# A four-layer mixer kernel: the first layer's dt block and first input block multiplied in the setup phase, its first B and C block split there

## The chip, the cores and the metric

The kernel runs on one core of one Trainium2 chip. The metric is the device time of one execution in microseconds (us), here the median of three. A core has five engines with queues of their own: TensorE multiplies matrices, VectorE, ScalarE and GpSimd work on elements, SyncE mostly issues transfers (DMA). The instructions of one engine run in order; the engines meet only at semaphores. In profile rows they are PE (PEld is its weight load), DVE, ACT, POOL and SP. A row with a q behind the engine, as SPq, is an instruction of its queue, such as the issue of a transfer.

## The reference

One prompt of 256 tokens and 8 samples of 4 tokens (288 columns in all) go through four layers. A layer is a root-mean-square norm, a mixer and a gated feed-forward part. The mixers are a state-space mixer (ssd), sliding-window attention, differential attention, and ssd again. The change touches only what comes before the first mixer and that mixer's start:

```python
for layer in range(DEPTH):
    hp = rmsnorm(xp, norm_mix[layer]); hs = rmsnorm(xs, norm_mix[layer])
    if kind == 0:                      # layers 0 and 3
        proj = h @ ssm_w_in            # z, x, B, C and dt columns: 2048 + 2048 + 512 + 512 + 32
        # causal convolution of width 4 over x, B, C, then silu; dt through softplus;
        # a state update per head from state_ssm; gate with z; norm; ssm_w_out
    x = x + mixer(h)
    x = x + swiglu(rmsnorm(x, norm_ffn[layer]), ffn_w_in[layer], ffn_w_out[layer])
```

All of it is float32. The kernel gets near that precision with numbers split in two: a rounded high part and the rest, so each product is three matmuls (high by high, low by high, high by low).

## The kernel before

The program is a row of phases. A phase ends when all five engines have reached its end, and the next begins with all of them together. The first is `setup`, then each layer has one phase or more.

Activations lie transposed: `x` is 8 chunks of 128 model features by 288 columns. `prepare` makes of each chunk the high part `xh` (ScalarE, L330) and the low part `xl` (VectorE, L336), and GpSimd adds up the squares in `acc` (L343 to L348). The norm's factor is applied behind the matmuls: `rstd` sums `acc` over the partitions on TensorE (L356) and ScalarE makes `rx` of it (L361, L365).

Weights come in blocks, numbered through the program. A block of 1 MB (0.5 MB for block 0) is loaded in two transfers into one of two buffers `raw` (L218), ScalarE rounds it into `whi` (`split_hi`, L229) and VectorE makes the rest `wlo` (`split_lo`, L240); `whi` and `wlo` have two buffers too. TensorE runs over it with `block_pieces`: 32 matmuls with `whi` (L268, 16 for block 0), then 16 with `wlo` (L276, 8 for block 0). The load of block g waits until the low part of block g-2 is made, the split of block g until TensorE is done with block g-2. All waits stand in the order of the code; nothing is scheduled by a program.

The first ssd layer takes its blocks in this order: 0 is the dt columns, 1 the first block of x, 2 to 5 the B and C columns, 6 the next of x, then z and x in turn. Between blocks TensorE does small work: `rs_pe` (L356), 24 transposes of the old convolution state (L951, of the tile `strow`), the transposes of dt (L957) and two products of the heads' constants (L960, L962). `strow` lies in the same memory as the first of the four state buffers `H`. So SyncE waits for `strow_turned`, which comes with the last of the 24 transposes, before it issues the four loads of `H` (512 KB each, L894), and behind these in its queue stand the loads of block 4 and block 5.

VectorE takes in this layer, in this order: three memsets (L1530 to L1532); dt scaled out of PSUM (L1538, which also frees PSUM bank 0 by the signal `out_read`); small work on constants; the old convolution state `stT` (L1551, waits for the 24 transposes); block 1 scaled into the convolution's buffer (L1509, L1511); the transposed dt (L1556); the low part of block 3; the convolution's taps (L1524); the softplus of dt; block 2 scaled; the low part of block 4 (L240); the rest of softplus up to `dsk` (L1581). With `dsk` TensorE may start the sums over tokens (L971), which stand in its queue ahead of block 4.

In `setup`, SyncE loads the table of constants `cst` (500 KB, with the identity in its first 128 columns) and the input `xt`, then blocks 0 and 1, then small rows of gains and convolution weights. TensorE waits for all of constants and input, transposes the input chunk by chunk (L635), then the rows (L641), then makes four distance tables (L650, each one matmul of 512 columns on 33 rows), which VectorE copies (L699) and SyncE stores. Last comes a small product whose copy is `lamcol` (L653, L713).

## Time and profile before

| what | us |
|---|---|
| median of 3 runs | 2025.04 |
| lowest and highest | 2024.25 and 2027.71 |
| the profiled execution | 2020.47 |
| its span | 2018.5 |
| TensorE busy | 1882.3 (93%) |
| VectorE busy | 1171.5 (58%) |
| ScalarE busy | 981.2 (49%) |
| GpSimd busy | 498.3 (25%) |

The span runs from the first instruction to the last; the profiled execution's own time is 2.0 us more. Times in rows count from the start of the span. Setup takes the first 32 us of it, the first layer's mixer begins there.

### The profile page before, as it was taken

The numbers are of one execution on the slowest core, as the hardware profiler recorded it, in microseconds if no ns is written. First come the engines' busy times: TensorE is split into PE (matmuls) and PEld (weight loads), VectorE is DVE, ScalarE is ACT, GpSimd is POOL, SyncE is SP. The second block draws the span as 40 slices with busy tenths as digits, with TensorE's granted clock in tenths as the row PEclk, the third lists the DMA queues.
The fourth block names the chain that finished last, engine by engine and source line by source line (L and its number), as shares of the span: only waits on it lengthen the run. The fifth ranks groups of instructions, "written<-read, shape, count | busy, mean of one in ns | idle before, by whom it ended". The sixth has DMA issues, their size and how long they took to land. (4 is left out here: it accounts for less than half of the span.)

```text
span 2018.5 us, 37752 instructions
## 1 busy us (share of the span) xinstructions
PE 1882.3 (93%) x14726; PEld 1770.9 (88%) x14726; DVE 1171.5 (58%) x2048; ACT 981.2 (49%) x1639; POOL 498.3 (25%) x521
## 2 busy tenths in 40 slices
PE   6899969999999979999897878999998999799999
PEld 4899959999998769999895658999988999699998
DVE  4678864555444356554446765555475888555544
ACT  3677763444343334443443554444347777544432
POOL 3122302343102113431103302343111222023320
PEclk9999979999999889999998998999998999799999
DMA  6367855555575536555657724655562787466544
GB/s 176 115 215 244 263 182 155 164 162 155 159 214 156 164 109 179 163 149 158 195 174 264 270 87 137 172 163 155 160 203 94 232 257 239 126 167 167 166 142 133
DMA packets 501554, 352.65 MB, mean 175 GB/s; under 512 B 14729, under 2 KB 486203, under 8 KB 500603
## 3 DMA queue, kind: packets, MB, share of 16 engines
q1 hardware_dynamic: 493508, 304.52, 52.0%
q0 software_dynamic: 7440, 45.43, 6.2%
q8 instruction: 118, 1.93, 0.4%
q14 instruction: 58, 0.48, 0.1%
q10 hardware_dynamic: 430, 0.29, 0.1%
HBM read 326.58 MB, written 50.63 MB: 187 GB/s over the span
## 5 line engine op out<-in xcount | busy, mean ns | idle before, releaser
L268 PE MATMUL ps<-xh,whi 128*128 128x288 f32 x2368 | 654.7, 302 | 10.1 <-PEq L176 9.9
L240 DVE TENSOR_TENSOR wlo<-raw,whi 128x2048 fp32r<-128x2048 f32 (+3 forms) x241 | 501.9, 2083 | 247.5 <-ACT whi L229 247.3
L268 PE MATMUL ps<-xl,whi 128*128 128x288 f32 x2368 | 643.8, 298 | 0.0
L229 ACT ACTIVATE whi<-raw 128x2048 fp32r<-128x2048 f32 (+3 forms) x241 | 419.1, 1740 | 265.8 <-PE ps L276 220.0
L268 PEld LDWEIGHTS ps<-xh,whi 128*128 128x128 f32 x2368 | 452.0, 191 | 12.7 <-issue 10.6
L268 PEld LDWEIGHTS ps<-xl,whi 128*128 128x128 f32 x2368 | 452.7, 191 | 0.8
L276 PE MATMUL ps<-xh,wlo 128*128 128x288 f32 x2368 | 353.2, 300 | 0.0
L276 PEld LDWEIGHTS ps<-xh,wlo 128*128 128x128 f32 x2368 | 327.1, 189 | 1.1
L526 POOL TENSOR_TENSOR gh<-sg,ut 128x288 f32<-128x288 f32 x88 | 216.2, 2457 | 353.1 <-ACT sg L467 353.1
L268 PE MATMUL ps<-hh,whi 128*128 128x288 f32 x704 | 189.7, 296 | 0.0
L268 PE MATMUL ps<-hl,whi 128*128 128x288 f32 x704 | 189.6, 297 | 0.0
L469 ACT ACTIVATE hh<-gh 128x288 fp32r<-128x288 f32 x88 | 39.2, 445 | 225.9 <-POOL gh L526 225.9
L268 PE MATMUL ps<-oh,whi 128*128 128x288 f32 x400 | 114.6, 312 | 33.2 <-DVE ol L399 18.1
L330 ACT ACTIVATE xh<-x,vec 128x288 fp32r<-128x288 f32 x64 | 33.9, 536 | 204.6 <-DVE x L486 123.0
L268 PEld LDWEIGHTS ps<-hl,whi 128*128 128x128 f32 x704 | 132.6, 188 | 0.0
L268 PEld LDWEIGHTS ps<-hh,whi 128*128 128x128 f32 x704 | 132.4, 188 | 0.0
L1230 POOL TENSOR_TENSOR E<-E,cb 128x288 f32<-128x288 f32 x64 | 58.5, 915 | 248.1 <-ACT E L1391 239.3
L268 PE MATMUL ps<-ol,whi 128*128 128x288 f32 x400 | 113.8, 309 | 0.0
L268 PEld LDWEIGHTS ps<-oh,whi 128*128 128x128 f32 x400 | 80.9, 202 | 35.5 <-issue 35.5
L276 PE MATMUL ps<-hh,wlo 128*128 128x288 f32 x704 | 104.2, 296 | 0.0
L503 DVE TENSOR_TENSOR hl<-gh,hh 128x288 fp32r<-128x288 f32 x88 | 40.3, 458 | 103.4 <-ACT hh L469 103.4
L345 POOL TENSOR_TENSOR sqx<-x 128x288 f32<-128x288 f32 x56 | 39.7, 710 | 245.6 <-DVE x L509 151.1
(326 smaller groups left out, 2658.2 us busy)
## 6 DMA issues: line engine op xcount, KB each, us to landing
raw<-in_ffn_w_in SPq DMA_DIRECT2D x176, 512.0 KB, 5.1
raw<-in_ssm_w_in SPq DMA_DIRECT2D x80, 512.0 KB, 5.2
raw<-in_ffn_w_out SPq DMA_DIRECT2D x64, 384.0 KB, 4.0
raw<-in_ffn_w_out SPq DMA_DIRECT2D x64, 320.0 KB, 3.2
H<-in_state_ssm SPq DMA_DIRECT2D x32, 512.0 KB, 4.6
out_ssm_sample<-H SPq DMA_DIRECT2D x32, 512.0 KB, 7.2
raw<-in_ssm_w_out SPq DMA_DIRECT2D x32, 512.0 KB, 5.3
Kp_L<-in_cache_diff_k SPq DMA_DIRECT2D x64, 256.0 KB, 4.5
```

The costliest lines, as they stand in the source:

```text
L229: act.activation(wts["hi"][:, s, 0:width], raw[:, s, 0:width], ACT.Copy).then_inc(hi_ready.sem, 1)
L240: dve.tensor_tensor(wts["lo"][:, s, 0:width], raw[:, s, 0:width], wts["hi"][:, s, 0:width].bitcast(F32), ALU.subtract).then_inc(lo_ready.s ...
L268: pe.matmul(out, W[0][:, kk, j, :], x_[:, k, :], stop=False, start=(part == 0 and kk == 0 and x_ is seg.hi), skip_group_check=True)
L276: mm = pe.matmul(out, W[1][:, kk, j, :], seg.hi[:, k, :], start=False, stop=(part == parts - 1 and end), skip_group_check=True)
L330: act.activation(th[:, c, :], x[:, c, :], ACT.Identity, scale=vec[:, 0, gain + c:gain + c + 1]).then_inc(xh_ready.sem, 1)
L345: pool.tensor_tensor(sqx[:, c % 2, :], x[:, c, :], x[:, c, :], ALU.mult).then_inc(sq_done.sem, 1)
L469: act.activation(hh[:, i, :], gh[:, r, :], ACT.Copy).then_inc(hid_hi.sem, hid_hi.inc())
L503: dve.tensor_tensor(hl[:, i, :], gh[:, r, :], hh[:, i, :].bitcast(F32), ALU.subtract).then_inc(hid_lo.sem, hid_lo.inc())
L526: pool.tensor_tensor(gh[:, r, :], sg[:, r, :], ut[:, r, :], ALU.mult).then_inc(gated_ready.sem, gated_ready.inc())
L1230: pool.tensor_tensor(E[:, h % 4, :], E[:, h % 4, :], cb[:, h // 8, :], ALU.mult).then_inc(w_ready.sem, w_ready.inc())
```

## The change

Setup gives the identity a transfer of its own, ahead of all; the input comes in two halves of 512 features, each with its own semaphore, and the rest of the constants behind the weights of blocks 0 and 1. The six small loads of `perhead` go from ScalarE's queue to SyncE's (`heads_in`). ScalarE loads its table of functions before the first chunk. TensorE then multiplies block 0 and block 1 in setup, with three of the tables between them and the norm's sum inside block 1; the fourth table, the transposes of the rows and `lamcol` come behind. ScalarE copies the tables in VectorE's place, makes `rx` and the high part of block 2; VectorE makes the low parts of blocks 0, 1 and 2. SyncE loads blocks 2 and 3 in setup. The first layer starts with block 2, and the 24 transposes and those of dt stand inside it. Layer 3 goes as before. The blocks' descriptions move out of `ssd` into `ssd_segs`, unchanged.

```diff
     def setup(nxt):
         stream["prep"] += 1
         prep_act, prep_dve, prep_pool = prepare(0, V_MIX)
+        rs_pe, rs_act, _ = rstd(stream["norm"])
+        opened = ssd_segs(0)
+        dt_seg, bc_seg, x_seg = opened
+        half, wide = D_MODEL // 2, 2 * KD * P
...
-            x_in = [(cst[:, :], A["constants"])]
-            x_in += [(xt[:, t, :], A["x_prompt"][0, t * P:(t + 1) * P, :]) for t in range(2)]
-            x_in.append((xt[0:NS, 2, :], A["x_sample"].rearrange("b t d -> (b t) d")))
+            x_in = []
+            for h in range(2):
+                cols = slice(h * half, (h + 1) * half)
+                x_in.append([(xt[:, t, cols], A["x_prompt"][0, t * P:(t + 1) * P, cols]) for t in range(2)])
+                x_in[h].append((xt[0:NS, 2, cols], A["x_sample"].rearrange("b t d -> (b t) d")[:, cols]))
...
             def _(sp):
-                for dst, src in x_in:
-                    sp.dma_start(dst, src).then_inc(x_loaded.sem, x_loaded.inc())
+                sp.dma_start(cst[:, 0:P], A["constants"][:, 0:P]).then_inc(ident_in.sem, ident_in.inc())
+                for h in range(2):
+                    for dst, src in x_in[h]:
+                        sp.dma_start(dst, src).then_inc(half_in[h].sem, half_in[h].inc())
                 for i in range(2):
                     load_block(sp, nxt, i, i, wait=False)
-                for dst, src in rows_in:
+                sp.dma_start(cst[:, P:], A["constants"][:, P:]).then_inc(cst_in.sem, cst_in.inc())
+                for dst, src in rows_in + heads_in:
                     sp.dma_start(dst, src).then_inc(rows_loaded.sem, rows_loaded.inc())
+                load_block(sp, bc_seg.lin, 0, 2)
                 sp.wait_ge(tab_moved.sem, tab_moved.at(4))
                 sp.dma_start(dist_tab.rearrange("k h n -> h k n"), tab[:, :, :]).then_inc(
                     tab_stored.sem, tab_stored.inc())
+                load_block(sp, bc_seg.lin, 1, 3)
...
+                block_mm(pe, dt_seg, 0)
+                pe.wait_ge(loaded.sem, loaded.at(len(rest_in)))
+                pe.wait_ge(made2.sem, made2.at(1))
+                for k in range(3):
+                    table(k)
+                L = block_pieces(pe, x_seg, 0)
+                for _ in range(KD):
+                    next(L)
+                pe.wait_ge(cst_in.sem, cst_in.at(1))
+                rs_pe(pe)
+                for _ in L:
+                    pass
+                pe.wait_ge(tab_moved.sem, tab_moved.at(1))
+                table(3)
...
                 for n in range(3):
-                    pe.transpose(ps[:, n, 0:used[n]], rows[0:used[n], n, :],
+                    pe.transpose(ps[:, 1, P * n:P * n + used[n]], rows[0:used[n], n, :],
                                  ident[0:used[n], 0:used[n]]).then_inc(turned.sem, turned.inc())
...
+                roots_table(act)
                 act.wait_ge(moved.sem, moved.at(1))
                 for c in range(KD):
                     act.wait_ge(turned.sem, turned.at(c + 2))
                     act.activation(x[:, c, :], ps[:, 3 + c % 4, 0:TOK], ACT.Copy).then_inc(x_done.sem, 1)
                     prep_act(act, c)
-                for i in range(2):
-                    split_hi(act, i, nxt.width if i else nxt.first_width)
+                split_hi(act, 0, nxt.first_width)
...
+                split_hi(act, 1, nxt.width)
+
+                def move_table(k):
+                    act.wait_ge(tab_made.sem, tab_made.at(k + 1))
+                    act.activation(tab[:, k, :], ps[0:NH, 4 + k % 3, :], ACT.Copy).then_inc(tab_moved.sem, tab_moved.inc())
+
+                for k in range(3):
+                    move_table(k)
+                rs_act(act)
+                move_table(3)
+                split_hi(act, 2, wide)
...
+                for n in range(3):
+                    lo = 0 if n else 32
+                    dve.tensor_copy(vec[:, n, lo:used[n]], ps[:, 1, P * n + lo:P * n + used[n]]).then_inc(
+                        moved.sem, moved.inc())
+                split_lo(dve, 2, wide)
...
-                for m in range(2, 4):
+                for m in range(2, 2 if opened else 4):
                     seg, i = block_of(m)
                     load_block(sp, seg.lin, i, b0 + m)
...
+                if opened:
+                    L = block_pieces(pe, bc_seg, 0)
+                    more(L, 4)
+                    turn_rows()
+                    more(L, 4)
+                    turn_dt()
+                    rows_of_heads()
+                    more(L, KD + 1)
+                else:
+                    block_mm(pe, dt_seg, 0)
+                    rs_pe(pe)
+                    turn_rows()
+                    block_mm(pe, x_seg, 0)
+                    turn_dt()
+                    rows_of_heads()
+                    block_mm(pe, bc_seg, 0)
...
-                rs_act(act)
+                if not opened:
+                    rs_act(act)
...
-        setup(firsts[0])
-        for layer in range(DEPTH):
+        opened = setup(firsts[0])
+        ssd(0, firsts[1], opened)
+        for layer in range(1, DEPTH):
             kinds[layer](layer, firsts[layer + 1])
```

TensorE at the boundary between setup and the first layer, before. The rows are the end of block 0 (`wlo`), the norm's sum, the transposes of `strow` (in the memory of `H`) and the first of block 1:

```order
L945 UNCONDITIONAL_BRANCH [waits barrier_Pool_Activation_PE_DVE_SP_release]
L268 MATMUL ps<-xh,whi 128x288 [waits x_lo_ready,weights_hi_ready]
...
L276 MATMUL ps<-xh,wlo 128x288 [waits weights_lo_ready]
L276 MATMUL ps<-xh,wlo 128x288 x7
L356 MATMUL ps<-acc,cst 128x288 [waits squares_added]
L951 MATMUL ps<-cst,H 128x24 [waits strow_in]
```

And in the changed kernel, where the first block of this phase is block 2:

```order
L680 MATMUL ps<-lw,cst 128x1 [waits moved,made]
L176 UNCONDITIONAL_BRANCH
L990 UNCONDITIONAL_BRANCH [waits barrier_Pool_Activation_PE_DVE_SP_release]
L268 MATMUL ps<-xh,whi 128x288 [waits x_lo_ready,weights_hi_ready,outs_read]
L268 MATMUL ps<-xl,whi 128x288
...
L995 MATMUL ps<-cst,H 128x24 [waits strow_in]
L995 MATMUL ps<-cst,H 128x24 x23
L268 MATMUL ps<-xh,whi 128x288 [waits x_lo_ready]
```

Ahead of the 24 transposes stood 24 matmuls of block 0 and the norm's sum; now 16 matmuls of block 2 stand there, and the first of these waits for `outs_read` (the signal `out_read`).

SyncE at the same boundary, before; `H` is first `strow`, then the states:

```order
L888 UNCONDITIONAL_BRANCH [waits barrier_Pool_Activation_PE_DVE_SP_release]
L890 DMA H<-in_state_ssm_conv 24x3072
L218 DMA raw<-in_ssm_w_in 128x4x256 [waits weights_lo_ready]
L218 DMA raw<-in_ssm_w_in 128x4x256
L894 DMA H<-in_state_ssm 128x8x128 [waits strow_turned]
L894 DMA H<-in_state_ssm 128x8x128 x3
```

And in the changed kernel, from the last small loads of setup on:

```order
L627 DMA perhead<-in_ssm_d 32x1 x2
L218 DMA raw<-in_ssm_w_in 128x4x256 [waits weights_lo_ready]
L218 DMA raw<-in_ssm_w_in 128x4x256
L630 DMA dist_tab<-tab 12x4x512 [waits tables_moved]
L933 UNCONDITIONAL_BRANCH [waits barrier_Pool_Activation_PE_DVE_SP_release]
L935 DMA H<-in_state_ssm_conv 24x3072
L939 DMA H<-in_state_ssm 128x8x128 [waits strow_turned]
L939 DMA H<-in_state_ssm 128x8x128 x3
L218 DMA raw<-in_ssm_w_in 128x4x256 [waits weights_lo_ready]
```

The loads of blocks 2 and 3 have gone ahead of the boundary; the states still wait for the 24 transposes, and block 4 still stands behind the states.

## Rows read from the trace of the kernel before

**Rows 1.** Head of the page: span and count.

```profile
span 2018.5 us, 37752 instructions
```

**Rows 2.** Waits of TensorE, 0 to 110 us: us, times, longest.

```profile
PE ps L630 <- DMA xt<-in_x_sample: 10.5, 1, 10.5
...
PE ps L971 <- DVE dsk L1581: 1.0, 1, 1.0
```

**Rows 3.** Busy per engine in stretches; then TensorE clock, DMA share, GB/s.

```profile
0.00:6.00 6.00, 0.00 (x0) 0.00 (x0) 0.13 (x2) 0.00 (x0) 0.20 (x4) 1.00 0.66 192
0.00:10.50 10.50, 0.01 (x1) 0.01 (x1) 0.15 (x3) 0.00 (x0) 0.20 (x4) 1.00 0.86 231
```

**Rows 4.** Timeline of setup: start us, us, engine, line, out<-in, count.

```profile
10.73 6.95 PE L635 MATMUL ps<-cst,xt 128*128 128x128 f32 x24
...
11.75 1.28 ACT L665 ACT_TABLE_LOAD   x1 [11.75 <-PE ps L635]
...
13.04 0.41 ACT L665 ACTIVATE x<-ps 128x288 f32<-128x288 f32 x1
...
17.87 0.83 PE L641 MATMUL ps<-cst,rows 101*128 101x101 f32 x3 [0.18 <-DMA rows<-in_diff_k_norm]
...
19.98 2.84 ACT L229 ACTIVATE whi<-raw 128x1024 fp32r<-128x1024 f32 x2
...
20.86 0.59 DVE L694 COPY vec<-ps 128x69 f32<-128x69 f32 x3
...
21.22 6.98 PE L650 MATMUL ps<-oh,rb 33*12 33x512 f32 x8 [2.52 <-DVE vec L694]
...
28.24 0.68 DVE L699 COPY tab<-ps 12x512 f32<-12x512 f32 x1 [1.03 <-PE ps L650]
...
31.80 0.16 DVE L713 COPY lamcol<-ps 128x1 f32<-128x1 f32 x1 [0.67 <-PE ps L653]
```

**Rows 5.** Timeline of the first layer's start, all engines.

```profile
32.42 0.58 PE L268 MATMUL ps<-xh,whi 128*128 128x288 f32 x1 [0.66 <-PEq L176]
...
33.20 0.91 DVE L1532 MEMSET Bm<- 32x1024 f32 x1 [0.16 <-issue]
...
36.36 1.22 PE L276 MATMUL ps<-xh,wlo 128*128 128x288 f32 x8
...
38.00 1.67 PE L951 MATMUL ps<-cst,H 24*128 24x24 f32 x24
...
39.11 0.46 DVE L1538 TENSOR_TENSOR G<-ps,rx 32x288 f32<-32x288 f32 x1 [5.00 <-ACT rx L365]
...
41.01 2.29 DVE L240 TENSOR_TENSOR wlo<-raw,whi 128x2048 fp32r<-128x2048 f32 x1 [0.75 <-ACT whi L229]
```

**Rows 6.** Timeline of SyncE's transfers, 39 to 47 us.

```profile
39.70 5.36 SPq L894 DMA_DIRECT2D H<-in_state_ssm  x4
45.10 2.60 SPq L218 DMA_DIRECT2D raw<-in_ssm_w_in  x2
```

**Rows 7.** Timeline of VectorE and ScalarE, 47 to 61 us.

```profile
47.05 0.21 DVE L1556 COPY G<-ps 128x64 f32<-128x64 f32 x1
...
53.97 1.92 ACT L229 ACTIVATE whi<-raw 128x2048 fp32r<-128x2048 f32 x1 [4.43 <-DMA raw<-in_ssm_w_in]
...
55.92 2.29 DVE L240 TENSOR_TENSOR wlo<-raw,whi 128x2048 fp32r<-128x2048 f32 x1
...
60.63 0.17 DVE L1581 COPY dsk<-ps 128x16 f32<-128x16 f32 x1
```

**Rows 8.** Stretches as in rows 3, later in the layer.

```profile
42.00:54.00 12.00, 12.00 (x94) 11.73 (x94) 9.17 (x17) 3.20 (x5) 0.77 (x4) 1.00 1.08 299
64.00:65.00 1.00, 1.00 (x6) 1.00 (x6) 1.00 (x3) 0.71 (x2) 0.68 (x1) 0.50 0.00 0
```

**Rows 9.** Timeline of TensorE, block 4.

```profile
63.44 0.48 PE L268 MATMUL ps<-xh,whi 128*128 128x288 f32 x1
...
69.32 2.32 PE L276 MATMUL ps<-xh,wlo 128*128 128x288 f32 x16
```

More of the change, by code:

```diff
@@ L707, in _ @@
                     made.sem, made.inc())
+                split_lo(dve, 0, nxt.first_width)
+                for q in range(2):
+                    rows_ = slice(32 * q, 32 * q + 32)
+                    dve.tensor_copy(id2[rows_, :], ident[rows_, rows_]).then_inc(filled.sem, filled.inc())
+                dve.tensor_copy(id2[2 * HEADS:P, :], ident[2 * HEADS:P, 0:HEADS]).then_inc(filled.sem, filled.inc())
                 dve.wait_ge(made.sem, made.at(3))
@@ L711, in _ @@
                     in1=lw[:, 2 * HD + 2:2 * HD + 3], op0=ALU.add, op1=ALU.subtract).then_inc(made.sem, made.inc())
+                split_lo(dve, 1, nxt.width)
+                dve.wait_ge(cst_in.sem, cst_in.at(1))
+                for q, (at, n) in enumerate(((C_TRI, P), (C_TRI, P), (C_TRIS, NS))):
+                    dve.tensor_scalar(after[:, q * P:q * P + n], cst[:, at:at + n], -1.0, -NEG, ALU.add,
+                                      ALU.mult).then_inc(filled.sem, filled.inc())
+                for n in range(3):
+                    dve.wait_ge(turned.sem, turned.at(KD + n + 2))
+                for n in range(3):
+                    lo = 0 if n else 32
+                    dve.tensor_copy(vec[:, n, lo:used[n]], ps[:, 1, P * n + lo:P * n + used[n]]).then_inc(
+                        moved.sem, moved.inc())
+                split_lo(dve, 2, wide)
                 dve.wait_ge(turned.sem, turned.at(KD + 5))
-                dve.tensor_copy(lamcol[:, :], ps[:, 7, 0:1]).then_inc(moved.sem, moved.inc())
+                dve.tensor_copy(lamcol[:, :], ps[:, 1, 500:501]).then_inc(moved.sem, moved.inc())
+        return opened
     def finish():
@@ L758, in ssd_first, with conv_of, ssd_segs, ssd @@
         return Linear(2, KD, 2, lambda i, slot: first(0, slot) if i == 0 else rest(i - 1, slot), KD * P)
-    def ssd(layer, nxt):
+    def conv_of(s):
+        return 4 + s if s else 0
+    def ssd_segs(layer):
+        w, early, b0 = A["ssm_w_in"][layer // 3], 4, stream["block"]
+        n_x, scaled = stream["prep"] - 1, S("xb_scaled")
+        at = lambda k: 8 * n_x + k + 1
+        dt = Seg(Linear(1, KD, 1, columns(w, KD, 1, col0=SSM_IN - P)), xh, xl, xl_ready, at,
+                 lambda o: (out_read, out_read.at(1)), places=[b0], banks=lambda i, j: 0)
+        bc = Seg(Linear(early, KD, 2, columns(w, KD, 2, col0=2 * D_INNER)), xh, xl, xl_ready, at,
+                 lambda o: (scaled, scaled.at(2 * (1 + o // 2) + 2)),
+                 places=[b0 + 2 + i for i in range(early)], banks=lambda i, j: 2 * (i % 2) + j)
+        xs = Seg(Linear(CI // 2, KD, 2, columns(w, KD, 2, col0=D_INNER)), xh, xl, xl_ready, at,
+                 lambda o: (scaled, scaled.at(2 * conv_of(o // 2) + 2)),
+                 places=[b0 + 1] + [b0 + 2 + early + 2 * i for i in range(CI // 2 - 1)],
+                 banks=lambda i, j: (2 if i == 0 else 0) + j)
+        return dt, bc, xs
+    def ssd(layer, nxt, opened=None):
         i_ssd = layer // 3
@@ L956, in _ @@
-                for t, n in TILES:
-                    mm = pe.transpose(ps[0:n, 6, 32 * t:32 * t + 32], dtT[:, cols_of(t)], ident[0:HEADS, 0:HEADS])
-                mm.then_inc(dt_turned.sem, dt_turned.inc())
-                pe.wait_ge(a_diag.sem, a_diag.at(2))
-                pe.matmul(ps[:, 7, 96:128], ones[0:HEADS, :], ea[:, 1:1 + HEADS], start=True, stop=True)
-                for h in range(2):
-                    mm = pe.matmul(ps[64 * h:64 * h + 64, 7, P:P + CI], ones[0:HEADS, 0:64], Dd[:, h, :],
-                                   start=True, stop=True)
@@ new lines, in rows_of_heads, with more @@
+                def rows_of_heads():
+                    pe.wait_ge(a_diag.sem, a_diag.at(2))
+                    pe.matmul(ps[:, 7, 96:128], ones[0:HEADS, :], ea[:, 1:1 + HEADS], start=True, stop=True)
+                    for h in range(2):
+                        mm = pe.matmul(ps[64 * h:64 * h + 64, 7, P:P + CI], ones[0:HEADS, 0:64], Dd[:, h, :],
+                                       start=True, stop=True)
+                    mm.then_inc(rows_mm.sem, rows_mm.inc())
+                def more(L, n=1):
+                    for _ in range(n):
+                        next(L, None)
@@ L1111, in turn_tail @@
                     mm.then_inc(tl_mm.sem, tl_mm.inc())
-                def more(L, n=1):
-                    for _ in range(n):
-                        next(L, None)
                 L = block_pieces(pe, *block_of(2 + EARLY))
```

87 lines of the change are left out of this document (30 added, 57 removed).

## The prediction

> **What bounds the kernel now.** I read the head of the page, then the waits of TensorE in the first 110 us, then timelines. The change touches only setup and the start of the first layer, so nearly all of the 2018.5 us span [rows 1] is out of its reach: it can only shift what comes behind it. TensorE waits 10.5 us for constants and input, and the only other wait in the stretch up to 61 us that the layer itself makes is 1.0 us for `dsk` at L971 [rows 2]. That small wait is the important one. TensorE is busy from 32.4 to 60 us, but where it arrives it still waits for VectorE, so the time of `dsk`, 60.63 + 0.17 = 60.8 us [rows 7], sets all that follows. Any gain has to come through `dsk`; TensorE's work ahead of it was nearly covered.
>
> What sets `dsk`? VectorE goes from the transposed dt at 47.05 to 60.8 without a long break [rows 7]. On the way stands the low part of block 4 at 55.92, which starts 0.03 us after its high part (53.97 + 1.92 = 55.89), and ScalarE began that one when the load of block 4 landed, after 4.43 us of idling for it [rows 7]. So there are two chains of nearly equal length: VectorE's own, and the transfer of block 4. The second begins with the 24 transposes: they end at 38.00 + 1.67 = 39.67, SyncE issues the four states at 39.70 and block 4 at 45.10 [rows 6], and block 4 is there at 53.97. From 42 to 54 us the DMA engines move 299 GB/s at a share over 1 [rows 8], which is 3.59 MB; four states and block 4 are 2.10 + 1.05 = 3.15 MB. This chain is filled by bytes, and takes 14.3 us from the end of the transposes (53.97 - 39.67).
>
> **The change, step by step.** I work out when the 24 transposes end, since block 4 follows by 14.3 us.
>
> *Input in halves.* All inputs, and the three tables on ScalarE's queue, are 1.92 MB; they were complete at 10.5 us, when 231 GB/s x 10.5 = 2.43 MB had moved [rows 2, 3]. Identity, first half and the same tables are 0.92 MB; with the same surplus (2.43/1.92) they are in when 1.16 MB have moved, and 192 x 6.0 = 1.15 MB had by 6.0 us [rows 3]. So transposing starts at 6.0 in place of 10.73 (bounds 5.3 and 7.5). The second half has until 9.5 and costs nothing. The function table, 1.28 us ahead of the first copy, is now loaded before. First copy: 6.0 + (13.04 - 10.73 - 1.28) = 7.0. ScalarE took from 13.04 to 19.98 for the eight chunks [rows 4]: done at 14.0. High part of block 0: about a third of 2.84 [rows 4], done at 14.9.
>
> *Block 0.* It took 32.42 to 36.36 for 16 matmuls, 0.246 us each [rows 5], at the half clock (at 63.44 to 69.32 block 4 shows the same pace until the clock comes back [rows 9], and there the clock column reads 0.50 [rows 8]; ahead of 60 us it reads 1.00 even at this pace, so I go by the pace). Here it again comes after transposes, which did not raise the clock before. 14.9 + 3.9 + 1.2 = 20.0.
>
> *Three tables.* Eight passes took 6.98 us at the half clock [rows 4]: three tables are 5.2, or 2.6 at the full clock. Then block 1: 32 matmuls are 5.9 when the clock must first come back, as for block 4 [rows 9], or 4.3 at the full clock; the norm's sum 0.7; 16 more 2.2 [rows 9]. I take the tables at 2.6, since dense work precedes them, and block 1 from the half clock: its end is 20.0 + 2.6 + 5.9 + 0.7 + 2.2 = 31.4 (29.8 if all is at full clock, 34.0 if neither is).
>
> *Tail of setup.* Fourth table 0.9; its copy, on ScalarE now, 0.6 (VectorE took 0.68); the high part of block 2 stands behind it, 1.9; its low part 2.3 [rows 5, 7]; `lamcol` 0.2, and 0.46 from its end at 31.96 to the first matmul of the layer at 32.42 [rows 4, 5]. The transposes of the rows (0.83) and their copies (0.59) [rows 4] run beside ScalarE's part. Sum 6.3, so the layer starts at 37.7 in place of 32.4. The small loads moved to SyncE's queue land long before they are needed.
>
> *Start of the layer.* Block 2 wants PSUM bank 0, which held dt; it is free when VectorE has scaled dt out, behind its three memsets. These ended 33.20 + 0.91 = 34.11, and scaling takes 0.46 [rows 5]: 2.2 us after the start. TensorE has then idled for some 5 us and begins at the half clock: 16 matmuls 3.9, then the 24 transposes 1.7. They end at 37.7 + 2.2 + 3.9 + 1.7 = 45.5, against 39.67: 5.8 us later.
>
> *What follows.* Blocks 2 and 3 are loaded early, but this takes no byte off the chain, because states and block 4 still start only behind the transposes and the earlier loads had just run dry when the states' data began. Block 4 lands at 45.5 + 14.3 = 59.8, its low part starts at 61.8, VectorE needs from there 60.8 - 55.92 = 4.9 to `dsk`: 66.6 in place of 60.8. VectorE's own chain would be ready sooner: dt transposed about 2.5 us behind the 24 transposes, at 48.0, and 13.3 us to `dsk` (13.75 less its short wait for block 3), 61.3. TensorE comes to L971 about 57 and now idles for some 9 us. Behind L971 every step takes its input from steps that have shifted alike, so I carry the shift to the end undiminished: +5.8.
>
> The load of block 5 is issued right behind block 4 now, since the low part of block 3 is long done. If the two shared the engines equally, block 4 could lose up to 1.5 us; if not, nothing. Before, 3.59 MB moved in 42 to 54 us where 3.15 were needed [rows 8], so some sharing was there already. The Trainium skill (DMA: Bandwidth & Descriptors, "Two DMAs through the same engine are not ordered") says that within one queue of one DMA engine descriptors start in order. By this rule block 5 takes nothing from block 4 and the shift stays; by the other bound it would be 1.5 us more. The surplus in the row stands for a mixture, and I add nothing.
>
> The sum is made against the profiled execution: 2020.47 + 5.8 = 2026.3. The median of the runs is 2025.04, 4.6 us above that execution; on it I expect **2030.9 us**, 0.29% slower.
>
> **Rivals.** *The transfer is not what is late.* If states and block 4 come 5 us faster than before from a queue that is empty, VectorE's own chain decides: `dsk` at 61.3, +0.5, or 2025.5. For it: VectorE's chain was as long as the transfer's. Against it: 3.15 MB in 9 us would be 350 GB/s from the first byte, and the stretch shows 299.
>
> *Faster: TensorE's queue decides.* Block 2 started at about 47 before (as dt was transposed, [rows 7]) and now at 37.7 + 2.2; the transposes inside are 1.7 + 0.8 and the slow clock 1.8, so TensorE comes some 2.8 us earlier, and up to 6 if setup ends at 35.5 with everything at the full clock. This counts only if `dsk` is not late, which the 1.0 us wait speaks against. Time: 2025.04 - 4.5 = 2020.5. The 4.7 us won on the input and 1.28 on the function table speak for a setup that is shorter than my sum.
>
> *Slower still.* Setup ends at 40.5 because tables and block 1 both run at the half clock, and block 5 takes its 1.5 us: +10, 2035.
>
> **How the numbers follow.** A change under 0.2%, 4 us, can't be told from none. My forecast has a chance of 0.54; its own range, from input at 5.3 and full clock to tables at the half clock, is +3 to +8, 2028 to 2033. Transfer in time 0.23, faster 0.11, slower still 0.12. Of the forecast some 0.06 lies under 4 us. So slower 0.60, same 0.28, faster 0.12. The range for 8 in 10 leaves out the faster case and half of the slowest one: 2025 to 2035.
>
> **What would show it.** In the profile of the changed kernel: the first transposes of input near 6 us; the first matmul behind the barrier near 40 us, with a wait for the scaled dt of about 2 us; the 24 transposes ending near 45.5 and the states issued at once; a wait of ScalarE for the load of block 4 that ends near 60; and a wait of TensorE at the first sum over tokens of 8 to 10 us for `dsk`. I am wrong if block 4 lands by 55, if setup ends before 36, or if the wait behind block 3 is there and a later stage gives it back.

## The result and the profile after

The changed kernel took 2027.93 us in the median of 20 runs (2018.98 to 2035.42), the kernel before 2021.01 us in 20 runs (2012.72 to 2027.84). The ratio is 1.0033 with a 95% interval of 1.0019 to 1.0047: slower by 6.7 us. The forecast was 5.8 us slower; the absolute time is 3 us lower than predicted because the kernel before, too, came out 4 us lower in 20 runs than in the first three of them. The interval is 3.8 to 9.5 us.

The head of the page after, and its waits of TensorE from 0 to 120 us (what waited, for whom, total, times, longest), to hold against [rows 1, 2]:

```profile
span 2031.2 us, 37759 instructions
```

The waits:

```profile
PE ps L1039 <- DVE dsk L1645: 9.2, 1, 9.2
PE ps L268 <- DVE G L1602: 5.8, 1, 5.8
...
PE ps L651 <- DMA xt<-in_x_sample: 3.3, 1, 3.3
PE ps L644 <- DMA cst<-in_constants: 3.0, 1, 3.0
```

The input wait of 10.5 us has become 3.0 for the identity and 3.3 for the first half. The wait for `dsk` has grown from 1.0 to 9.2 us, and a new one of 5.8 us stands at block 2, for the scaled dt. The prediction had some 9 us for the first, and for the second 2.2 us behind the layer's start, after some 5 of idling; the row counts both together, from TensorE's last work in setup.

Setup, one timeline (start, duration, engine, line, out<-in); it answers to [rows 4]; `whi` at 14.61 is the high part of block 0:

```profile
6.64 6.95 PE L651 MATMUL ps<-cst,xt 128*128 128x128 f32 x24 [3.31 <-DMA xt<-in_x_sample]
...
7.67 0.41 ACT L693 ACTIVATE x<-ps 128x288 f32<-128x288 f32 x1 [3.71 <-PE ps L651]
...
14.61 1.04 ACT L229 ACTIVATE whi<-raw 128x1024 fp32r<-128x1024 f32 x1
...
21.08 2.74 PE L656 MATMUL ps<-oh,rb 33*12 33x512 f32 x6
...
22.14 0.59 ACT L703 ACTIVATE tab<-ps 12x512 f32<-12x512 f32 x1 [3.44 <-PE ps L656]
```

And its end, with the start of the layer, as in [rows 5]; the first rows are ScalarE's high part and VectorE's low part of block 2:

```profile
30.83 1.02 PE L656 MATMUL ps<-oh,rb 33*12 33x512 f32 x2
...
32.39 1.89 ACT L229 ACTIVATE whi<-raw 128x2048 fp32r<-128x2048 f32 x1
...
34.31 2.29 DVE L240 TENSOR_TENSOR wlo<-raw,whi 128x2048 fp32r<-128x2048 f32 x1 [1.27 <-ACT whi L229]
36.52 0.15 DVE L750 COPY lamcol<-ps 128x1 f32<-128x1 f32 x1
...
37.92 0.91 DVE L1596 MEMSET Bm<- 32x1024 f32 x1 [0.16 <-issue]
...
38.86 0.46 DVE L1602 TENSOR_TENSOR G<-ps,rx 32x288 f32<-32x288 f32 x1
...
39.37 0.61 PE L268 MATMUL ps<-xh,whi 128*128 128x288 f32 x1 [5.83 <-DVE G L1602]
...
43.51 1.90 PE L995 MATMUL ps<-cst,H 24*128 24x24 f32 x24
```

The layer starts at 37.1 in place of 32.4, the first matmul of block 2 waits until the dt is scaled out, at 38.86 + 0.46, and the 24 transposes end at 45.4.

SyncE, ScalarE and VectorE from there on, as in [rows 6, 7], each engine's timeline by itself:

```profile
45.45 4.06 SPq L939 DMA_DIRECT2D H<-in_state_ssm  x4
```

```profile
59.45 1.91 ACT L229 ACTIVATE whi<-raw 128x2048 fp32r<-128x2048 f32 x1 [10.24 <-DMA raw<-in_ssm_w_in]
```

```profile
48.04 0.23 DVE L1620 COPY G<-ps 128x64 f32<-128x64 f32 x1 [1.11 <-PE ps L1002]
...
61.40 2.29 DVE L240 TENSOR_TENSOR wlo<-raw,whi 128x2048 fp32r<-128x2048 f32 x1 [4.86 <-ACT whi L229]
...
66.11 0.17 DVE L1645 COPY dsk<-ps 128x16 f32<-128x16 f32 x1
```

The states are issued at 45.45, the moment the transposes end, block 4 lands 14.0 us later (14.3 before), ScalarE has then idled for 10.2 us, and VectorE for 4.9 us behind it. `dsk` is there at 66.3 in place of 60.8.

So far the trace is the prediction's. Two things more are in it. TensorE's clock in stretches of the changed kernel (the clock is the third number from the end; 0.50 is 1.2 GHz, 1.00 is 2.4):

```profile
56.00:58.00 2.00, 1.19 (x9) 0.95 (x8) 0.54 (x2) 0.00 (x0) 0.36 (x2) 1.00 1.10 348
60.00:61.00 1.00, 0.00 (x0) 0.00 (x0) 0.00 (x0) 1.00 (x1) 0.00 (x0) 1.00 0.24 76
62.00:63.00 1.00, 0.00 (x0) 0.00 (x0) 1.00 (x1) 0.98 (x2) 0.00 (x0) 0.50 0.00 0
67.00:71.00 4.00, 4.00 (x18) 2.98 (x18) 4.00 (x8) 1.23 (x3) 1.20 (x1) 0.50 0.33 116
```

TensorE was done with block 3 at 57.2, and by 62 the clock had gone to half. So the sums over tokens, which stand between `dsk` and block 4, ran at the half clock and took 66.43 to 70.75, 4.3 us, where the kernel before took 2.5 us, 60.95 to 63.44 [rows 9]. TensorE at the start of the sums before, then at their start and at block 4 after:

```profile
60.95 0.38 PE L971 MATMUL ps<-G,cst 128*128 128x32 f32 x2 [0.96 <-DVE dsk L1581]
```

```profile
66.43 0.61 PE L1039 MATMUL ps<-G,cst 128*128 128x32 f32 x2 [9.23 <-DVE dsk L1645]
...
70.75 0.61 PE L268 MATMUL ps<-xh,whi 128*128 128x288 f32 x1
```

The shift grows from 5.5 at `dsk` to 7.3 at block 4. And the first state-space chunk in steady work (the first write of its output tile `yt`, 112.1 before) comes at 123.9, 11.8 us late: there another 4.2 us come in. The stretches below, of 4 us each, begin 8 us behind the first transposes of the convolved x, which stand at 80.0 before and 87.57 after; first the kernel before, then the changed one:

```profile
88.00:92.00 4.00, 1.44 (x7) 1.44 (x8) 3.30 (x7) 3.76 (x12) 0.00 (x0) 0.86 0.15 49
92.00:96.00 4.00, 3.12 (x18) 2.54 (x17) 1.01 (x3) 3.43 (x7) 0.65 (x4) 0.71 0.00 0
96.00:100.00 4.00, 4.00 (x31) 3.52 (x31) 0.00 (x0) 2.95 (x9) 1.23 (x2) 1.00 0.02 4
```

```profile
95.57:99.57 4.00, 1.45 (x8) 1.45 (x9) 3.31 (x7) 3.80 (x12) 0.00 (x0) 0.89 0.15 50
99.57:103.57 4.00, 2.95 (x14) 2.31 (x13) 1.01 (x3) 3.16 (x6) 0.65 (x4) 0.50 0.00 0
103.57:107.57 4.00, 4.00 (x18) 3.23 (x18) 0.00 (x0) 1.35 (x6) 0.00 (x0) 0.50 0.01 4
```

In both TensorE waits 3.7 us there for ScalarE. Before, the clock is at half for about 3 us behind that wait; after, for more than 8 us in a row, though TensorE is busy for most of the time. The twelve traces of this study fall into two groups at this place: from the first transposes of x to the first `yt` they take 32.0 to 32.1 us (the kernel before, and e3, e6, e7, e8 below), or 35.1 to 36.6 us (the changed kernel, e1, e2, e4, e5, e9, e10). e4 is the kernel before but for one load, so the old order can have the long stretch too.

A second such place is block 1 in setup. Its first 32 matmuls take 4.3 us where all are at the full clock (the changed kernel, e5, e9), and 5.9 where about half are at 1.2 GHz (e1, e2, e6, e7, e8, e10); with the later start of the tables there this makes the layer start 2.3 to 3.1 us later with the same instructions: 37.1 and 36.9 against 39.6, 39.4 and 40.0 (e1, e2, e8). The profiled span of the changed kernel is 12.7 us longer, and 11.8 of it are there at the first `yt`, the long stretch with them; the comparison of 20 runs gives 6.7. Behind the first `yt` all twelve traces run the same code, and yet they take 1897.8 to 1910.1 us for it. That is why I read the experiments below stage by stage, counted from the layer's start: one profile's span can't tell a change of 5 us.

### The profile page after: what moved, and what is told of

Read it like the earlier page. It is cut to its first block and busy times, and to the rows that moved or that the text cites. A ratio compares the mean times of both kernels' runs of the same rounds, so it can differ in the third digit from the quotient of the medians.

```text
span 2031.2 us, 37759 instructions
## 1 busy us (share of the span) xinstructions
PE 1886.6 (93%) x14726; PEld 1776.5 (87%) x14726; DVE 1171.3 (58%) x2044; ACT 982.3 (48%) x1642; POOL 497.2 (24%) x521
## 5 line engine op out<-in xcount | busy, mean ns | idle before, releaser
L268 PEld LDWEIGHTS ps<-oh,whi 128*128 128x128 f32 x400 | 80.5, 201 | 35.5 <-issue 35.5
```

The costliest lines, as they stand in the source:

```text
L268: pe.matmul(out, W[0][:, kk, j, :], x_[:, k, :], stop=False, start=(part == 0 and kk == 0 and x_ is seg.hi), skip_group_check=True)
```

## The experiments

Theory A is the prediction's: the 24 transposes of the convolution state, now 16 matmuls and a wait deep in the layer, release the states, behind these comes block 4, and that makes `dsk` late. Theory B: setup has become too long and TensorE starts at the half clock; block 4 only looks late. The table gives, from each profile, where the layer starts (the first instruction of VectorE), the end of the 24 transposes, the start of ScalarE's split of block 4, the end of `dsk`, the first matmul of block 4 (all in us), and the ratio of times to the kernel before.

| run | layer starts | transposes end | block 4 split | dsk | block 4 matmul | ratio, 95% interval |
|---|---|---|---|---|---|---|
| before | 32.4 | 39.7 | 54.0 | 60.8 | 63.4 | 1 |
| changed | 37.1 | 45.4 | 59.5 | 66.3 | 70.8 | 1.0033 (1.0019 to 1.0047) |
| e1 block 4 first | 39.6 | 47.7 | 53.2 | 63.6 | 68.1 | 1.0028 (1.0013 to 1.0043) |
| e2 rows first | 39.4 | 45.8 | 59.3 | 66.1 | 70.6 | 1.0037 (1.0014 to 1.0059) |
| e3 halves alone | 29.4 | 36.9 | 50.9 | 58.0 | 60.6 | 0.9968 (0.9949 to 0.9987) |
| e4 before, block 4 first | 32.0 | 40.0 | 53.9 | 61.1 | 63.7 | 1.0005 (0.9986 to 1.0025) |
| e5 memsets late | 36.9 | 44.3 | 57.9 | 64.7 | 69.2 | 1.0023 (0.9998 to 1.0049) |
| e6 tail early | 35.5 | 44.0 | 57.7 | 64.5 | 69.0 | 1.0025 (1.0004 to 1.0046) |
| e7 reordered | 35.6 | 43.5 | 48.1 | 56.5 | 59.1 | 0.9970 (0.9949 to 0.9991) |
| e8 filler | 40.0 | 48.1 | 62.1 | 69.0 | 71.6 | 1.0002 (0.9982 to 1.0022) |
| e9 block 3 early | 33.3 | 41.7 | 48.6 | 55.5 | 58.1 | 0.9977 (0.9959 to 0.9995) |
| e10 the same, filler | 35.4 | 43.3 | 47.8 | 55.8 | 59.1 | 0.9947 (0.9928 to 0.9966) |

In e5, e7, e9 and e10 the memsets are not VectorE's first work; there the layer's start is that of the scaling of dt.

The last two columns go together in most runs: the shift of block 4's first matmul against the 63.4 of the kernel before lies inside the interval of the measured time in all but e8 and e10. These are the two runs with filler matmuls, and they are some 8 and 6 us faster than the shift says. In e8 `dsk` is 8.2 us later than in the kernel before, and the time is the same (1.0002). So the lateness of `dsk` by itself does not give the time of the whole kernel: filling the wait behind it brought some 6 us in the timed runs. Its profile shows 3.6 of them in the clock behind the wait (e8 below), and it has no long stretch at half clock later on; whether that is the filler's doing is not shown, as e10 has the filler and the stretch.

**e1: block 4 ahead of the states, in the changed kernel.**

```diff
+                if opened:
+                    load_block(sp, bc_seg.lin, 2, b0 + 4)
                 sp.wait_ge(strow_turned.sem, strow_turned.at(1))
                 for c in range(4):
                     load_state(c)
-                for m in range(4, 9):
+                for m in range(5 if opened else 4, 9):
```

> The changed kernel, with one edit: in the first layer SyncE issues the load of block 4 ahead of the wait for the 24 transposes and of the four states, not behind them. Theory A (block 4's transfer, held back by the late transposes, is what makes dsk late): ScalarE no longer waits until 59.5 us for block 4 but starts its high part as soon as TensorE is done with block 2, near 51; VectorE's wait of 4.9 us for it is gone; dsk comes at 48.0 + 13.3 = 61.4, as VectorE's own chain has it, in place of 66.3. The kernel is 4.9 us faster than the changed kernel, that is 1 to 2.5 us slower than the kernel before (ratio 1.0005 to 1.0013). Theory B (the layer is late because setup ends late and TensorE starts at the half clock; block 4 only looks late): dsk stays within 1 us of 66.3 and the ratio within 0.05% of the changed kernel's 1.0033.

ScalarE's and VectorE's timelines at block 4:

```profile
53.19 1.92 ACT L229 ACTIVATE whi<-raw 128x2048 fp32r<-128x2048 f32 x1 [1.71 <-PE ps L276]
```

```profile
50.31 0.22 DVE L1622 COPY G<-ps 128x64 f32<-128x64 f32 x1 [1.09 <-PE ps L1004]
...
58.72 2.28 DVE L240 TENSOR_TENSOR wlo<-raw,whi 128x2048 fp32r<-128x2048 f32 x1
...
63.43 0.17 DVE L1647 COPY dsk<-ps 128x16 f32<-128x16 f32 x1
```

ScalarE waits 1.7 us for TensorE and not at all for the transfer, VectorE goes through without a wait. From the layer's start to `dsk` it takes 24.0 us, where the changed kernel takes 29.2: 5.2 us less, forecast 4.9. Theory A holds for the stage, B would have left 29.2. The ratio of times doesn't show it: 1.0028, where 1.0005 to 1.0013 was expected, 1 us less than the changed kernel in place of 4.9. In this profile setup took 2.5 us longer with the same instructions, since the clock went to half in the middle of block 1 (above), and TensorE still waited 4.3 us for `dsk`, so that the sums again ran at the half clock (63.75 to 68.1); the interval is 3 us wide either way. Block 4's transfer is worth 5 us inside the stage; that the whole kernel gains as much is not shown by this run.

**e2: the 24 transposes ahead of block 2.**

```diff
                 if opened:
-                    L = block_pieces(pe, bc_seg, 0)
-                    more(L, 4)
                     turn_rows()
-                    more(L, 4)
+                    L = block_pieces(pe, bc_seg, 0)
+                    more(L, 8)
```

> The changed kernel, with one edit: the 24 transposes of the convolution state stand ahead of block 2, not inside it. Theory A: they end when their rows have landed, some 3 us behind the layer's start at 37.1, plus 1.9, so near 42 in place of 45.4. Block 4 follows them by 14.1, so ScalarE starts on it near 56, dsk comes near 63 (66.3 now), and the ratio to the kernel before falls to about 1.0015. VectorE's own chain (61.4) isn't reached. Theory B (the chain through the transposes doesn't matter): the transposed dt comes no earlier, so dsk and ratio stay as in the changed kernel.

TensorE's waits of e2, 0 to 120 us:

```profile
PE ps L995 <- DMA H<-in_state_ssm_conv: 7.1, 1, 7.1
```

Its timeline and its clock (third from the end) at the transposes:

```profile
43.00 2.75 PE L995 MATMUL ps<-cst,H 24*128 24x24 f32 x24 [7.14 <-DMA H<-in_state_ssm_conv]
```

```profile
43.00:45.70 2.70, 2.70 (x25) 2.65 (x25) 0.00 (x0) 0.68 (x1) 0.00 (x0) 0.50 0.00 0
```

The rows of the convolution state, issued at 39.3, were there only at 43.0, and the transposes behind them ran at the half clock, 2.75 us in place of the 1.9 I had counted. They ended 6.4 us behind the layer's start, not 4.9 as I had it; in the changed kernel it is 8.3. Block 4 followed them by 13.5, and `dsk` came 26.7 behind the start, 2.5 less than 29.2 (expected 3.3). The direction is A's, the size smaller, and the ratio (1.0037 for some 1.0015) shows nothing of it.

**e3: the input part alone, on the kernel before.** The diff is that of the change for `x_in`, the identity, the rest of the constants and the early function table, with VectorE's `after` moved behind the low parts:

```diff
+                sp.dma_start(cst[:, 0:P], A["constants"][:, 0:P]).then_inc(ident_in.sem, ident_in.inc())
+                for h in range(2):
+                    for dst, src in x_in[h]:
+                        sp.dma_start(dst, src).then_inc(half_in[h].sem, half_in[h].inc())
...
+                roots_table(act)
                 act.wait_ge(moved.sem, moved.at(1))
```

> The kernel before, with the input part of the change alone: identity first, input in halves, the other constants behind blocks 0 and 1, and ScalarE's function table loaded early. By the time of the input alone, all of setup would move 4.1 + 1.3 = 5.4 us ahead (ratio 0.9973). Against it: SyncE's queue issues the small rows no earlier, they landed at 17.9 us before, and TensorE's transposes of them stand ahead of the tables, VectorE's copies of them ahead of the low parts of blocks 0 and 1. By that, TensorE waits 4 us for them at 13.7, the tables start where they did, and the layer starts within 1 us of before: ratio 0.9995 to 1.000. I hold the second for the likelier.

The forecast that I held for the likelier was wrong: this part alone makes the kernel faster. The ratio, 0.9968 (0.9949 to 0.9987), agrees with the other one, 0.9973, but the trace doesn't: the layer starts 2.9 us earlier, at 29.4, and not 5.4. TensorE waited 3.2 us for the small rows, much as I had it. But the rows were there at 17.08 in place of 17.87, and the tables followed at once, at 17.92 in place of 21.22: before, they had waited another 2.5 us for VectorE's copies of the rows [rows 4], which came behind its low parts of the input, and these are now done earlier. That wait is what I had left out.

TensorE's timeline of e3 at the first table:

```profile
17.92 6.98 PE L660 MATMUL ps<-oh,rb 33*12 33x512 f32 x8
```

Everything behind moves by about as much: block 4 is split at 50.9, 3.1 us earlier, and `dsk` ends at 58.0, 2.8 us earlier. No other part of the change was tested alone on the kernel before. Against this one the changed kernel loses 8 us at `dsk`.

**e4: block 4 ahead of the states, in the kernel before.** The edit is that of e1, for the first layer.

> The kernel before, with block 4's load ahead of the states in the first layer. In the kernel before VectorE began the low part of block 4 only 0.03 us behind its high part, so both chains were equally long. Theory A: block 4 lands by 50, ScalarE starts its high part when TensorE is done with block 2 (53.4, now 53.97), VectorE is not there before 55.92, dsk stays at 60.8, and the time is within 0.5 us of before. If the transfer alone had bounded dsk there, it would come up to 3 us earlier (ratio 0.9985).

ScalarE at block 4 in e4, then VectorE, then the last matmuls of block 2 in the kernel before:

```profile
53.93 1.92 ACT L229 ACTIVATE whi<-raw 128x2048 fp32r<-128x2048 f32 x1 [4.10 <-PE ps L276]
```

```profile
56.21 2.28 DVE L240 TENSOR_TENSOR wlo<-raw,whi 128x2048 fp32r<-128x2048 f32 x1
```

```profile
51.26 2.32 PE L276 MATMUL ps<-xh,wlo 128*128 128x288 f32 x16
```

`dsk` ended at 61.1 (60.8), the ratio is 1.0005. In the kernel before the transfer cost nothing, since ScalarE may split block 4 only when TensorE is done with block 2, at 53.6 there and 53.9 here, and VectorE comes to it without a wait at 55.9 and 56.2. The same edit gives 5 us in the changed kernel: a wait that was covered came out when the work covering it moved away.

**e5: the memsets behind dt.** The three `dve.memset` lines of the layer go behind the last work on constants.

> The changed kernel, with VectorE's three memsets at the layer's start put behind the scaling of dt and the small work on constants. TensorE's first matmul of block 2 waits for that scaling, which now ends 2.2 us behind the layer's start. Theory A: it ends 0.5 to 0.6 us behind the start, all of TensorE's work, the 24 transposes, states and block 4 move ahead by 1.7 us, and from the layer's start (VectorE's first memset in the changed kernel, its first instruction there) to the end of dsk it takes 27.5 us in place of 29.2. Rival: the rows of the convolution state land some 4 us behind the start, but 16 matmuls at the half clock cover that in both, so they don't matter; if the transfer of block 4 didn't depend on TensorE, 29.2 would stay.

From the layer's start (36.9) to `dsk` 27.8 us, expected 27.5: the wait at PSUM bank 0 had cost 1.4 us. The first matmul of block 2 came the full 1.8 us earlier, 0.5 behind the start. But the 24 transposes, at the half clock to their end, took 2.75 us in place of 1.90, as in e2; block 4 followed them by 13.6 in place of 14.0. The ratio, 1.0023 (0.9998 to 1.0049), can't be told from the changed kernel's.

**e6: the tail of setup into the gaps.**

```diff
                 for k in range(3):
                     move_table(k)
-                rs_act(act)
-                move_table(3)
                 split_hi(act, 2, wide)
+                move_table(3)
+                rs_act(act)
```

TensorE's fourth table and row transposes move between block 1's parts in the same way, VectorE's low part of block 2 ahead of its copies.

> The changed kernel, with the tail of setup moved into the gaps: the fourth table and the three transposes of the rows go between block 1's two parts, ScalarE makes block 2's high part ahead of the fourth table's copy and of rx, VectorE its low part ahead of the copies of the rows. In the changed kernel 6.3 us pass from the end of block 1 to the layer's start, and 1.8 of them are TensorE's. By theory A, which has setup's end on the path, the layer starts at 33 to 34 us (35.5 to 36.5 where TensorE's clock comes back later in setup) in place of 37.1 (39.5), all behind shifts by the same 3.5 us, and the ratio is about 1.0015. If the transfer of block 3, which starts behind the fourth table too, or something else took the place of the tail, the gain would be under 1.5 us.

VectorE's timeline of e6 at the end of setup:

```profile
27.05 2.29 DVE L240 TENSOR_TENSOR wlo<-raw,whi 128x2048 fp32r<-128x2048 f32 x1 [4.49 <-ACT whi L229]
...
32.08 0.61 DVE L747 COPY vec<-ps 128x69 f32<-128x69 f32 x3 [2.39 <-PE ps L672]
34.95 0.16 DVE L750 COPY lamcol<-ps 128x1 f32<-128x1 f32 x1 [2.26 <-PE ps L680]
35.51 0.30 DVE L1594 MEMSET acHL<- 64x288 f32 x1 [0.40 <-PEq L176]
```

This trace has the slow block 1, and the layer starts at 35.5, where e1 and e2, with the same block 1, have 39.6 and 39.4: 4 us, as forecast for this case. VectorE's low part of block 2 now lies inside the time that it waited. From the layer's start to `dsk` it is 29.0 us, as in the changed kernel (29.2), so the 4 us are kept. The ratio, 1.0025, is 0.0008 below that of the changed kernel, less than the 0.0018 expected, within intervals of 0.002 either way.

**e7: all of it.** Beside e1, e5 and e6, TensorE transposes dt ahead of block 2, and VectorE begins on it and on block 3's low part ahead of the copy `stT`:

```diff
                 if opened:
-                    L = block_pieces(pe, bc_seg, 0)
-                    more(L, 4)
-                    turn_rows()
-                    more(L, 4)
                     turn_dt()
                     rows_of_heads()
-                    more(L, KD + 1)
+                    L = block_pieces(pe, bc_seg, 0)
+                    more(L, 4)
+                    turn_rows()
+                    more(L, KD + 5)
```

> All that theory A asks for, in one kernel: the tail of setup as in the run before, the memsets behind dt, block 4 ahead of the states, the transposes of dt and the heads' products ahead of block 2, and VectorE's first work on the transposed dt and the low part of block 3 ahead of the copy of the convolution state. The layer starts at 33 to 36. VectorE has then some 20 us of work to dsk: dsk near 55 (60.8 in the kernel before, 66.3 in the changed one). TensorE arrives there 18 to 19 us behind the layer's start, so its wait is under 2 us and the sums over tokens run at the full clock. 5 to 6 us faster than the kernel before, ratio 0.9970 to 0.9976. Rival: the chain through ScalarE (taps behind the split of block 3, whose load starts late) takes the place; then 1 to 3 us faster.

TensorE at the first of the sums:

```profile
56.62 0.38 PE L1040 MATMUL ps<-G,cst 128*128 128x32 f32 x2 [2.27 <-DVE dsk L1652]
```

`dsk` ended at 56.5, 20.8 us behind the layer's start (20 expected), 9.8 us earlier than in the changed kernel and 4.3 earlier than before; TensorE waited 2.3 us for it (under 2 expected), and the sums ran at the full clock, 56.62 to 59.1. The ratio is 0.9970 (0.9949 to 0.9991). It does the same work as the changed kernel in another order, and is faster than the kernel before: what the change lost was in its order.

**e8: 62 matmuls to fill the wait.** They multiply two constant tiles into a free bank, and their results are not used:

```diff
                 block_mm(pe, bc_seg, 1)
+                if opened:
+                    pe.wait_ge(strow_moved.sem, strow_moved.at(1))
+                    for _ in range(62):
+                        pe.matmul(ps[:, 5, 0:TOK], idr[:, :], after[:, :], start=True, stop=True, skip_group_check=True)
```

> The changed kernel, with 62 extra matmuls of 288 columns behind block 3, where TensorE waits 9.2 us for dsk; their results are not used. At the full clock they take 8.3 us. They change no other engine's work, so dsk stays 29.2 us behind the layer's start. What they tell is the cost of the half clock: without them the sums over tokens take 4.3 us (2.5 in the kernel before) and block 4 starts at the half clock. If the idle time is the cause, the sums take 2.5 us or less, and block 4's 48 matmuls 6.4 to 8 us in place of 8.0. If the sums are slow for another reason (their operands, the semaphores), 4.3 us stay.

TensorE's timeline at that place, and its clock (third from the end) in two stretches:

```profile
59.73 8.43 PE L1038 MATMUL ps<-after,idr 128*128 128x288 f32 x62
69.09 0.38 PE L1043 MATMUL ps<-G,cst 128*128 128x32 f32 x2 [0.94 <-DVE dsk L1649]
...
71.42 0.24 PE L1045 MATMUL ps<-cst,G 32*32 32x32 f32 x2
```

```profile
59.00:68.00 9.00, 9.00 (x69) 8.92 (x67) 3.99 (x9) 5.86 (x7) 0.59 (x3) 1.00 0.53 159
71.60:75.00 3.40, 3.40 (x27) 3.40 (x26) 3.40 (x6) 2.15 (x5) 2.54 (x2) 1.00 0.02 5
```

`dsk` came 28.9 us behind the layer's start, as expected. The sums took 69.09 to 71.59, 2.5 us, against 4.3, and block 4's first 32 matmuls 71.59 to 75.94, 4.4 us, against 6.2 in the changed kernel and 5.9 before [rows 9]. From `dsk` to the first transposes of x it is 17.7 us, against 21.3 in the changed kernel and 19.2 before. So the idle time at `dsk` cost 3.6 us by the clock, on top of the wait itself. The ratio is 1.0002 against 1.0033, some 6 us less, more than these 3.6; the intervals overlap by a hair. The mean clock of the timed runs is 0.967 in e8's ten and 0.963 in the changed kernel's twenty.

**e9 and e10: block 3 early, without and with a filler of 20.** On e7, `load_block(sp, bc_seg.lin, 1, 3)` goes ahead of the wait for the tables; e10 has 20 matmuls as in e8 besides.

> The reordered kernel, with the load of block 3 ahead of the distance table's store in SyncE's queue. In the reordered kernel block 3 was issued at 32.7 us, ScalarE waited for it until 39.8, and VectorE stood still for 1.6 us at its low part. Now it is issued near 23 and lands by 30: ScalarE splits it at the layer's start. Theory A: dsk 2 to 3 us earlier, 18.5 us behind the layer's start in place of 21.2, and the ratio to the kernel before 0.9955 to 0.9965. If TensorE (block 2 done 12 us behind the start) takes the bound, the gain is under 1 us.

> The same as the run beside it, with 20 extra matmuls of 288 columns behind block 3, 2.7 us at the full clock, where TensorE waits for dsk. If that wait is 2 us or more and the clock falls behind it, the sums and block 4 gain up to 1.8 us from the clock; if the wait is shorter than 2.7 us the extra matmuls stand in the way and cost the difference, up to 2.7 us. I expect a wash: within 1 us of the run beside it.

TensorE's and ScalarE's waits of e9, 30 to 100 us:

```profile
PE ps L1040 <- DVE dsk L1652: 0.7, 1, 0.7
```

```profile
ACT whi L229 <- PE ps L276: 4.0, 1, 4.0
```

In e9 `dsk` came 22.2 us behind the layer's start, no sooner than in e7 (20.8) and far from the 18.5 forecast: ScalarE now waits 4.0 us for TensorE to be done with block 2 before it can split block 4. This is the case where TensorE takes the bound; but in e9 its clock stood at half from 36.8 to 47.0, in e7 only from 38.9 to 42.3, so the two don't compare block 3's load alone. e10 does, with its clock at half from 38.2 to 41.7: there `dsk` came 20.4 behind the start, 0.4 us sooner than in e7. Block 3's load was not what held e7. In e9 the first transposes of x came at 73.2, the earliest of all, as block 1 had the full clock and block 4 too; then came the long stretch at half clock at the next wait, and the first `yt` stood at 109.6, against 107.7 in e7. The ratio, 0.9977, is no better than e7's. e10 filled more than the wait (`dsk` at 55.8, the sums at 56.64), and its ratio is the best of all, 0.9947 (0.9928 to 0.9966), some 6 us under e9's where a wash within 1 us was expected. Up to the first `yt` its trace is no better than e9's (109.2 and 109.6, the same long stretch in both). Behind it, where the code is the same, it takes 1901.0 us against 1907.6, and the timed runs of e10 have a higher mean clock, 0.9685 against 0.9659; what brings that is not shown, and the intervals touch. Both beat the kernel before and the changed kernel.

## Why the prediction was right

- *What bounds.* That `dsk` sets what follows in the layer, and that the transfer had been covered before and was not after, holds: e4 takes it away in the kernel before and nothing happens, e1 takes it away in the changed kernel and 5.2 us of the stage go. Two chains to `dsk` were equally long, but ScalarE's split of block 4 hung on a third thing that the prediction doesn't name, TensorE's end of block 2 at 53.6, 0.4 us ahead of the transfer.
- *Input.* Forecast 6.0, measured 6.64 for the first half; ScalarE was through the chunks at 14.6 for 14.0.
- *Block 0, tables, block 1.* The sum had the end of block 1 at 31.4. It was 30.8 where the clock stayed up through block 1, and 33.3 in e1 where it went down at 25.5 and came back at 28.9. That 31.4 and 30.8 are so close is in part luck: block 0 ended 1.1 us later than in the sum (21.1 for 20.0), and block 1's first 32 matmuls, which I had from the half clock, took 4.3 for 5.9. The tables ran at the full clock, as I had them (2.6, measured 2.74). The bounds, 29.8 to 34.0, cover both traces.
- *Tail of setup.* 6.3 us; measured 30.83 to 37.08, 6.25.
- *Start of the layer.* 2.2 + 3.9 + 1.7 us to the end of the transposes, 7.8; measured 8.3 (2.3 + 4.1 + 1.9). Their end: 45.5 forecast, 45.4 measured, since the layer started at 37.1 for 37.7 and made up for it.
- *Block 4.* 14.3 us behind it; measured 14.0. Block 5 was issued right behind block 4 (SyncE issued both in one go, 49.6 to 55.1), and block 4 was no later for it; the bound of 1.5 us was not used. That is what the rule of the Trainium skill would give (DMA: Bandwidth & Descriptors, "Two DMAs through the same engine are not ordered"), by which the descriptors in one queue of one DMA engine start in order. The order itself this trace doesn't show: from 45.41 to 59.45 the DMA engines moved 280 GB/s, 3.9 MB, where states and block 4 are 3.15, so other bytes, of block 5 or small ones, moved ahead of block 4's last.
- *dsk.* 66.6 forecast, 66.3 measured; TensorE's wait 9 forecast, 9.2 measured.
- *"I carry the shift to the end undiminished."* This is the step that failed in part. It did not shrink, it grew: the sums over tokens ran at the half clock, 1.8 us more, a term that isn't in my sum although I had written that TensorE would idle for 9 us. In the profiled execution 4.2 us more came at the next wait. The measured 6.7 us agree with the 7.3 at block 4, and their interval, up to 9.5, has no room for all of the 4.2. How often the long stretch comes in timed runs of either kernel stays open: they show only the mean clock of the whole run. That 5.8 forecast and 6.7 measured lie so close is in part luck: the term at `dsk` was right in the profile, the 1.8 at the sums was missing, and e8, with `dsk` as late, is no slower than the kernel before.
- *The rivals.* "The transfer is not what is late" is refuted by ScalarE's wait to 59.45 and by e1. "TensorE's queue decides" is refuted by the 9.2 us wait; setup was shorter than the sum, as it has it, but by 0.6 us and not by 2. "Slower still" had a part in it: its layer start of 40.5 is near the 39.4 to 40.0 of e1, e2 and e8, though there the tables ran at the full clock and only block 1 did not, and block 5 took nothing.

## What to carry to other kernels

Work moved ahead of a boundary pays only if what it leaves behind is also released earlier: look for each transfer that waits on a small job of the moved stretch (here the four states and block 4, on 24 transposes), and issue the one that is needed first ahead of it. Before moving work off an engine with little idle time, see whose slowness that work had covered; e4 and e1 are the same edit, worth nothing in the one kernel and 5 us in the other. And test the parts alone: the input part (identity first, input in halves, function table early) was worth a third of a per cent, and the rest of the change hid it.

## What the runs showed of the hardware

- An idle TensorE can cost twice. In the changed kernel the clock read 1.00 from 56 to 58 us, 0.50 by 62, after the last matmul at 57.2; the small float32 matmuls behind took 4.3 us where they take 2.5. 62 matmuls without use in that gap gave 3.6 us back. In e7, where the wait was 2.3 us, the same matmuls took 2.5.
- The same 0.95 us gap in front of the same small matmuls was followed by the half clock in the kernel before (63.4 to 66.9) and not in e8 (clock 1.00 from 71.6 to 75). Behind the same wait of 3.7 us, five traces lost nothing more and seven lost 3 to 4.5 us to a longer stretch at 1.2 GHz, and the same instructions of setup differ by 2.3 to 3.1 us. What decides isn't shown by these runs; it is more than most edits here give.
- A transfer of 24 rows of 12 KB took 3.7 us from issue to use in e2, behind the load of block 3 in the same queue, on which ScalarE waited until 41.8; from 41.8 to 43.0 the DMA engines moved next to nothing (0 GB/s).
- 24 small transposes (24x24) took 1.67 us at the full clock (e1, the kernel before), 2.75 us at half (e2, e5), and 1.90 where the clock rose among them (the changed kernel).
